# First attention of a two-block kernel: convolution taps dealt out anew between narrow and wide slots, and the causal mask added by VectorE instead of by a product

## What is computed

```python
# attention of the first block: c is the running sum of the forget gate's logarithm
s = jnp.einsum("bhqd,bhkd->bhqk", qi, kh).astype(jnp.float32) * scale
s = s + ci[..., :, None] - c[:, :, None, :]
s = jnp.where(k_pos[None, :] <= q_pos[:, None], s, -jnp.inf)
p = jax.nn.softmax(s, axis=-1)
out = jnp.einsum("bhqk,bhkd->bhqd", p, vh)
# convolution of the first block, 512 channels, 31 taps
a = a_in[..., :CONV_CH] * jax.nn.sigmoid(a_in[..., CONV_CH:])
a = lax.conv_general_dilated(a, w, (1,), [(30, 0)], feature_group_count=CONV_CH) + b
```

## Time and profile before

| | before |
|---|---|
| median of 3 runs | 2784.43 us (2783.95 to 2786.92) |
| the profiled execution's own time | 2781.31 us |
| span of the profile | 2780.0 us |
| TensorE busy | 2643.0 us, 95% |
| VectorE busy | 1838.4 us, 66% |
| ScalarE busy | 1274.2 us, 46% |
| GpSimd busy | 486.1 us, 17% |

### The profile page before, as it was taken

How to read it: one execution, slowest core, us unless ns; L and a number is a source line. 1 busy time by engine, 2 the same in 40 slices (tenths; PEclk the granted TensorE clock), 3 DMA queues, 4 the chain that set the end, 5 groups by cost and what they waited for, 6 DMA issues and landing times. The chain is left out here.

```text
span 2780.0 us, 35577 instructions
## 1 busy us (share of the span) xinstructions
PE 2643.0 (95%) x13421; PEld 2212.0 (80%) x13421; DVE 1838.4 (66%) x2261; ACT 1274.2 (46%) x1918; POOL 486.1 (17%) x661
## 2 busy tenths in 40 slices
PE   8999999999999999999999999989999599999995
PEld 7788788888897877777888898868877488888884
DVE  4278766643437887875556533389845788888887
ACT  4144344241224333333444312178732377777774
POOL 4323220000003222222011220012232300000102
PEclk9999999999999999999999999999999799999998
DMA  8321120111322445566764532000233699999996
GB/s 274 125 69 36 64 65 16 46 53 51 116 76 88 137 144 170 177 195 218 254 190 151 156 76 68 13 20 20 80 130 138 242 379 393 396 395 395 396 396 235
DMA packets 248745, 461.88 MB, mean 166 GB/s; under 512 B 15820, under 2 KB 137408, under 8 KB 247168
## 3 DMA queue, kind: packets, MB, share of 16 engines
q1 hardware_dynamic: 218752, 354.83, 36.4%
q0 software_dynamic: 29712, 104.75, 11.3%
q10 hardware_dynamic: 112, 0.03, 0.0%
HBM read 384.79 MB, written 65.32 MB: 162 GB/s over the span
## 5 line engine op out<-in xcount | busy, mean ns | idle before, releaser
L502 PE MATMUL ps<-r,r 128*128 128x512 f32 (+2 forms) x10316 | 2273.8, 379 | 21.0 <-DVE r L1984 5.2
L502 PEld LDWEIGHTS ps<-r,r 128*128 128x128 f32 x10316 | 1851.1, 189 | 370.3 <-issue 11.0
L479 ACT ACTIVATE r<-f 128x2048 fp32r<-128x2048 f32 (+2 forms) x339 | 504.4, 1494 | 400.3 <-PE ps L502 392.2
L3699 DVE TENSOR_TENSOR r<-f,r 128x2048 fp32r<-128x2048 f32 x188 | 429.2, 2291 | 63.7 <-ACT r L479 62.6
L487 DVE TENSOR_TENSOR r<-f,r 128x1024 fp32r<-128x1024 f32 (+1 forms) x151 | 169.1, 1132 | 337.8 <-ACT r L479 337.5
L502 PE MATMUL ps<-f,f 128*128 128x64 f32 (+3 forms) x1410 | 219.8, 305 | 1.7 <-ACT f L1246 1.4
L502 PEld LDWEIGHTS ps<-f,f 128*128 128x128 f32 (+1 forms) x1410 | 180.9, 193 | 24.6 <-issue 21.0
L872 DVE SCALAR_TENSOR_TENSOR f<-f,misc,f 128x1023 f32<-128x1023 f32 (+29 forms) x120 | 155.8, 1340 | 0.0
L1977 ACT ACTIVATE r<-f 128x512 fp32r<-128x512 f32 x140 | 87.4, 629 | 81.9 <-PE ps L502 57.4
L1162 ACT ACTIVATE f<-ps,misc 128x128 f32<-128x128 f32 (+7 forms) x64 | 47.5, 742 | 153.3 <-DVE misc L1151 153.3
L3717 POOL DMA_INDIRECT ff_scratch<-f,misc x15 | 28.8, 1917 | 474.4 <-ACT f L3828 412.2
(11 more groups left out here) (342 smaller groups left out, 2187.6 us busy)
## 6 DMA issues: line engine op xcount, KB each, us to landing
f<-in_w_gate_dram SPq DMA_DIRECT2D x64, 1024.0 KB, 8.4
f<-in_w_up_dram SPq DMA_DIRECT2D x64, 1024.0 KB, 10.1
f<-in_w_down_dram SPq DMA_DIRECT2D x64, 1024.0 KB, 8.1
f<-in_w_in_dram SPq DMA_DIRECT2D x56, 512.0 KB, 4.5
f<-in_w_ada_dram SPq DMA_DIRECT2D x48, 512.0 KB, 5.0
f<-in_w_ffn_in_dram SPq DMA_DIRECT2D x80, 256.0 KB, 4.1
hid_scratch<-f POOLq DMA_DIRECT2D x77, 256.0 KB, 3.7
f<-hid_scratch SPq DMA_DIRECT2D x35, 512.0 KB, 5.3
```

Of the source, the lines that this page charges most:

```text
L479: self.act.activation(hi, raw, ACT.Copy).then_inc(self.sem(st.name + "_hi"), 1)
L502: return self.pe.matmul(o, left, right, start=start, stop=stop, skip_group_check=True)
L3699: self.dve.tensor_tensor(es.lo[i % 4], es.raw[i % 8], es.hi[i % 4].bitcast(F32), ALU.subtract).then_inc(self.sem("e_lo"), 1)
```

## The change

Two things. First, TensorE's product with the mask is gone, and `dve_largest` begins with an addition of the mask to the last 128 columns of the scores, in the accumulator, and waits for its end before it takes the maximum. The rounded copy of the mask, ScalarE's instruction that made it, and its count in `round` go too. Second, the taps of a slot: in slots 12 to 14 and 1 to 3 of each 16 there are three, one ahead of `dve_copy_p` and two behind it; in slots 4 to 11 one. Before there were two in each slot but 12 and 14, where there was one. Slots 15 and 0 have none, as before. The sum over 16 slots is 26 either way.

```diff
--- before.py
+++ after.py
@@ -39,7 +39,7 @@
      ("v2_mm", 16), ("cv2_mm", 24), ("a2_pT", 96), ("rt_mm", 8), ("aff_T", 4), ("top_T", 1), ("AB_mm", 1),
      ("xs_T", 32), ("last_up", 1)),
     (("at_pTd", 32), ("ffg_mm", 4), ("a2_oT", 32), ("o2_mm", 8), ("hi_T", 32)),
-    (("round", 2), ("n1_sq", 8), ("pj_v", 32), ("a2_val", 32), ("hi_hi", 32)),
+    (("round", 1), ("n1_sq", 8), ("pj_v", 32), ("a2_val", 32), ("hi_hi", 32)),
     (("w_hi", 143), ("a2_exp1", 32)),
     (("n1_hi", 16), ("glu_sig", 8), ("cf", 1), ("fgT", 2), ("fg_a", 2), ("pj_sq", 32), ("a2_sq", 32), ("xm_a", 8),
      ("aff_exp", 2), ("h7_a", 1), ("e_hi", 192)),
@@ -166,8 +166,7 @@
         self.base = base = (nc.sbuf_base + 31) // 32 * 32
         self.misc = nc.alloc_sbuf_tensor_at("misc", [P, MISC], F32, offset=base + 201 * 1024)
 
-        self.ident_r, self.mask_r = [nc.alloc_sbuf_tensor_at(f"round{j}", [P, P], F32R, offset=base + 201 * 1024 + j * P * 4)
-                                     for j in (0, 3)]
+        self.ident_r = nc.alloc_sbuf_tensor_at("round0", [P, P], F32R, offset=base + 201 * 1024)
         self.ident = self.ident_r[:, 0:P].bitcast(F32)
         self.ps = self.ctx.enter_context(nc.psum_tensor("ps", [P, 8, 512], F32))
         dram = lambda n, *shape: nc.dram_tensor(n, shape, F32, kind="Internal").ap()
@@ -635,7 +634,6 @@
 
         act.wait_ge(*sem("consts", 6))
         act.activation(self.ident_r[:, 0:P], self.eye, ACT.Copy).then_inc(sem("round"), 1)
-        act.activation(self.mask_r[:, 0:P], self.mask, ACT.Copy).then_inc(sem("round"), 1)
         for i in range(6):
             square(i)
             if i == 3:
@@ -703,7 +701,7 @@
 
         pe.wait_ge(*sem("consts", 4))
         self.pe_keep_busy(15, 6)
-        pe.wait_ge(*sem("round", 2))
+        pe.wait_ge(*sem("round", 1))
         pe.wait_ge(*sem("rows", 128))
         pe.transpose(ps[:, 7, 0:56], self.rows_a[0:56, :], ident[0:56, 0:56]).then_inc(sem("cols_T"), 1)
         self.pe_keep_busy(5, 6)
@@ -1011,11 +1009,14 @@
                 self.dve_scale(g, u)
             if tg is not None:
                 self.dve_normed(tg, t)
+            wide = 12 <= s % 16 <= 14 or 1 <= s % 16 <= 3
+            if wide:
+                self.dve_taps(1)
             g, u = self.unit(s, 1)
             if g is not None and u >= 8:
                 self.dve_copy_p(g, u)
             if s % 16 not in (0, 15):
-                self.dve_taps(2 if s % 2 or s % 16 <= 10 else 1)
+                self.dve_taps(2 if wide else 1)
 
 
 
@@ -1136,11 +1137,8 @@
             pe.wait_ge(*sem("glu", 6))
         for c0 in range(0, kw, 512):
             w = min(512, kw - c0)
-            diag = c0 + w == kw
             o = self.ps[:, b0 + c0 // 512, 0:w]
-            m = self.mm(o, self.QT[0:66, h, i * P:(i + 1) * P], self.KT[0:66, h, c0:c0 + w], True, not diag)
-            if diag:
-                m = self.mm(o[:, w - P:w], self.ident_r[:, 0:P], self.mask_r[:, 0:P], False, True)
+            m = self.mm(o, self.QT[0:66, h, i * P:(i + 1) * P], self.KT[0:66, h, c0:c0 + w], True, True)
         m.then_inc(sem("at_qk"), 1)
 
     def dve_largest(self, g, u):
@@ -1148,8 +1146,11 @@
         dve.wait_ge(*sem("at_qk", 16 * g + u + 1))
         if u >= 2 or g:
             dve.wait_ge(*sem("at_exp", 16 * g + u - 1))
-        dve.tensor_reduce(self.nmax[u % 2], self.scores_of(u)[1], AX.X, ALU.max, negate=True).then_inc(
-            sem("at_max"), 1)
+        scores = self.scores_of(u)[1]
+        diagonal = scores[:, self.UNITS[u][0] * P:]
+        dve.tensor_tensor(diagonal, diagonal, self.mask, ALU.add).then_inc(sem("at_mask"), 1)
+        dve.wait_ge(*sem("at_mask", 16 * g + u + 1))
+        dve.tensor_reduce(self.nmax[u % 2], scores, AX.X, ALU.max, negate=True).then_inc(sem("at_max"), 1)
 
     def act_exp(self, g, u):
         act, sem = self.act, self.sem
```

## The result

The kernel with the change takes **2796.18 us** in the median of 12 runs (2781.26 to 2804.53), the one before 2782.93 in 12 runs on the same chip: a ratio of 1.0045, 95% interval 1.0035 to 1.0056, so 12.5 us (10 to 16) slower. The profiled execution of the changed kernel took 2794.64.

The account below looks back on a forecast made before the run. TensorE bounds the first attention (busy 355.39 of 375 us), with VectorE's maximum on a chain without slack. Terms -3.8 + 8.6 + 4.6 + 3.4 - 5 - 4.4 + 7.5 = +10.9 on 2784.4 give 2795.3 us, range 2785 to 2803.

Parts of the forecast that it names:

- -3.8 + 8.6: First attention: 64 mask products removed from TensorE, -3.8 us; the addition's 0.33 in 26 slots waiting for ScalarE's copy, +8.6.
- the narrow slots' sum: Narrow slots: -2.7 and -3.3 from fewer taps, +2 for additions, -1 for three covered wide slots; -5 us (-9 to -1).
- the rival of a dearer addition: VectorE's mask addition takes 0.45 us: 3.1 more, 2798.4 us; inside the forecast's own range, no separate chance.
- The product's 0.06: TensorE's cost per mask product, read at unit 7's score passes: 0.06 us, not the 0.3 to 0.6 of its record.
- the start +3.4: First group's slots 1 to 3: an extra tap each makes the second tile's mean squares late, +3.4 us (2.5 to 4).
- unit 10's tap: Slot 14: a second tap behind the copy delays unit 11's maximum, 1.2 in three groups, 1.0 in the fourth; +4.6 us.
- unit 2's wait of 0.97: Fourth group, q/k transposes: only 0.5 us of this wait was VectorE's lateness, the rest the way over GpSimd and ScalarE.
- the narrow slots decide: Rival: one tap in narrow slots removes the q/k transposes' waits; 14 us won, 2778.8 us without clock falls; chance 0.1 (faster).
- The second group, forecast -4.4: A late weight load comes in time: its 1.42 us wait and the clock fall behind it go, -1.4 - 3 = -4.4.
- The clock, forecast +7.5: New falls to half clock: start 1.5, group two 3, one of unit 11's slots in groups one and three 3; 0 to 13.
- no new falls: Rival: transposes and products break up the waits of 1.8 and 2.5 us, so no clock fall; 2787.8 us; chance 0.2.
- weight loads late in every group: Rival: loads land 1.2 us late, three groups each repeat the second group's 4.4; 2803 us; chance 0.13, shared with more falls.

Follow-up runs that it names:

- mask_only: The changed kernel with the taps dealt as before the change, so only the mask's addition is new: 2793.68 us, ratio 1.0046 to the kernel before.
- taps_only: The kernel before with the change's new taps, the mask still a product: 2781.87 us, ratio 0.9999 to the kernel before.
- start_two: The changed kernel with two taps in each of the loop's first three slots: 2788.13 us, ratio 1.0023 to the kernel before.
- add_twice: The changed kernel with each mask addition made twice in a row: 2812.41 us, ratio 1.0107 to the kernel before.
- after_again: The changed kernel unaltered, run again for a second profile and more times: 2793.70 us, ratio 1.0042 to the kernel before.
- shift: The kernel before with 33 filler products on TensorE at the end of this attention, 7.2 us of delay: 2788.03 us, ratio 1.0028.
- product_best: The kernel before, mask still a product, with taps re-dealt by what the earlier runs showed: 2774.60 us, ratio 0.9971.

## Why the prediction came out right, and where it was not

The total (2795.3 against 2796.18, stage +10.9 against 12.0) was right, and so was the place: the chain of scores, maximum, exponential, copy and transposes. Even the split between work and clock holds: without the clock the forecast is 10.9 - 7.5 + 3 = 6.4 and the profiles say 7.7, and the clock's terms, 7.5 - 3 = 4.5, come to 4.3 by the same estimate. (The step between the medians is 12.5 and not 10.9; the times agree to 0.9 because before's own median came out 1.5 lower than the 2784.43 on which the forecast was built.) But within the work two terms were off in opposite directions, so that the total is right partly by luck.

**The mask, forecast +5.8 by its own terms, measured 12.8 (9 to 16).** The terms are -3.8 + 8.6, and out of the narrow slots' sum +2 for additions there and -1 for three of the 26. The duration was right (298 ns and 0.03 between, forecast 0.33 together; the rival of a dearer addition falls). The counts were not. In the wide slots the forecast nets 8.6 - 1 - 1.9 = 5.7; in mask_only the slots of units 8 to 15, unit 12's of the second group with its fall of the clock left out, are 8.4 longer together. It let the addition count only in the 26 slots whose transposes are listed with a wait, less three; in fact most of the wide slots grew by 0.25 to 0.35, and the last three by 0.1. In the narrow slots it nets 2 - 1.9, about nothing: six slots pay, and all 32 get the product back. Measured are twelve that pay, 4.6 together, and eleven, those that TensorE bounds, that get back 0.1 each: +3.6. The product's 0.06, read from one place, is under the 0.1 of those eleven. 8.4 + 3.6 = 12.0.

The sentence "Minimize op *count*, not sems" (Trainium skill, "VectorE: DVE Perf Modes", "Rules for kernel authors") fits this half: an operation of 0.3 us more in the chain of a wide slot costs about 0.3 us, 2.56 of idle time ahead of it notwithstanding. What the semaphore between addition and maximum costs by itself no run here shows. The same page of the Trainium skill gives 258 ns in its section on the TRN2 errata, an estimate for this size; the addition measured 298.

**The taps, forecast +5.1 with the clock (4.6 + 3.4 - 6 - 4.4 + 7.5), measured 0 (-2.8 to +2.5).** Single terms were good: the start +3.4 (3.9 in the first slot of after; 0.95 of wait instead of 3.79 once undone), unit 10's tap 1.2, 1.2, 1.2 and 1.0 (in taps_only 1.2, 1.2 and 0.8 outside the second group). The mean squares at the start came at 144.20, a little ahead of the 144.7 that the prediction gave as the earliest. The **narrow slots** were mis-sized: the taps' part of my -5 was -6, and taps_only shows -10.0; the kernel after, with the additions in these slots, -8.0. The forecast took 0.5 of unit 2's wait of 0.97 for VectorE's lateness; the whole of it was. This is the rival "the narrow slots decide" in part: it was right in its mechanism, and short of the 14 from which it would have decided.

**The second group, forecast -4.4.** Unit 12's slot is 4.1 shorter in the kernel after, as forecast, but not because a load came in time: unit 11's slot before it grew by 2.1 and holds the wait, 3.14 us. That it brought no fall of the clock was this execution's luck. In taps_only, start_two, add_twice and after_again a wait of 3.0 to 3.2 us stands there, and the fall with it.

**The clock, forecast +7.5 for new falls, less 3 for the one of before.** In the first profile of after two stretches of 3.4 us, at the start and in group three; in the second four, 20.5 us in all; against 6.8 and 3.4 us in the two of before. Half of the difference of the means is the 4.3 above. The rival "no new falls" (2787.8) is out as the usual case. Two of the twelve runs took 2781.26 and 2783.97, at a mean granted clock of 0.984 and 0.982, where the rest have 0.974 to 0.979; whether they had no fall in this stage isn't known, as they have no profile. The rival "weight loads late in every group" (2803) falls too: apart from stretches at half clock, unit 12's slots grew by no more than the addition. Its own sum is also short: three groups at 4.4 make 13, not 8.

**Behind the stage** the prediction said that no weight load is tied to a fixed time. The delay of shift fits that (7.8 for 7.2). For a gain it stays open: product_best won 5 us less at its end than in the stage, and before's own two profiles differ by 4.5 there.

## What to carry to other kernels

Moving an operation off the busiest engine pays only if the receiving engine has slack at that point of the chain; VectorE was busy 278 of 375 us and idle 2.56 us right ahead of the addition, and in the wide slots it still cost nearly its full 0.3 us. A removed instruction is credited only where its own engine bounds the slot, an added one is charged where it stands on the chain that the slot waits for: here in nearly all wide slots and in twelve of the 32 narrow ones. Filler work with no due time (the taps) belongs behind the chain's last VectorE step and ahead of a known idle time, never ahead of an operation that somebody waits for: dealing it better was worth 8 us with no other instruction changed. And where the clock can fall, two profiles of one kernel should be read, and half of the half-clock time taken off, before a few us in one of them are explained: in this stage that left two profiles of one kernel within 0.5 us, where they had differed by 7.

## What the runs showed of the hardware

- The same wait of TensorE (3.14, 3.15, 3.15 and 3.16 us, at one place of the program in after, after_again, add_twice and start_two) went with no fall of the granted clock, with 3.4, with 10.2 and with 13.7 us at 0.50. The prediction reasoned from the length of waits (1.99 fell, 1.48 didn't); the length alone doesn't decide. What else does stays open. In unit 11's slot of the first group the wait of 1.89 went with no fall in after and start_two and with 10.2 us at 0.50 in after_again.
- VectorE adding 128x128 in place in the accumulator takes 298 ns, where reading it from there and writing to SBUF takes 285, and a dependent second one follows 0.04 us behind the first.
